# A mixture-of-experts block on one core: down weights laid out by pieces, no barrier behind the last round, the last norm inside the loop

## What is computed

```python
top_val, top_idx = lax.top_k(logits, TOP_K)
gates = jax.nn.softmax(top_val, axis=-1)
...
hid = xb @ w_mlp1[e] + b_mlp1[e]
glu = jnp.minimum(hid[..., ::2], SWIGLU_LIMIT)
lin = jnp.clip(hid[..., 1::2], -SWIGLU_LIMIT, SWIGLU_LIMIT)
act = glu * jax.nn.sigmoid(SWIGLU_ALPHA * glu) * (lin + 1.0)
return act @ w_mlp2[e] + b_mlp2[e]
...
out = jax.ops.segment_sum(y, slot_tok, num_segments=n + 1)[:n]
...
x = x + gt2 * rms_norm(ffn, g_post_ffn[l])
```

## Time and profile before

| | us |
|---|---|
| three runs: median (lowest, highest) | 1760.31 (1758.86, 1767.95) |
| the profiled execution | 1761.02 |
| its span, first to last instruction | 1759.2 |
| PE, PEld, DVE, ACT busy | 1606.3, 887.2, 620.0, 351.0 |
| L898 / L931 products, busy (2048 / 1024 records) | 456.5 / 234.1 |
| L920, second passes (128 records, 1157.4 to 1365.0) | 27.8 |
| loads of expert weights | 384, 1 MB each |
| tail, small ones: L2177 total, L1424 root, L2180 reciprocal | 0.16, 0.30, 0.17 |
| tail: a Square of a quarter with the read of its total (L1419) | 0.69 |

### The profile page before, as it was taken

One profiled execution on the slowest core, in us unless ns is written; L12 is line 12 of the kernel. 1 busy time (PEld: TensorE's weight loads), 2 busy tenths in 40 slices (PEclk: granted clock), 3 DMA queues, 4 the chain that ended last, 5 costly groups with the idle time before them and its releaser, 6 DMA issues. The chain is left out here.

```text
span 1759.2 us, 20527 instructions
## 1 busy us (share of the span) xinstructions
PE 1606.3 (91%) x7254; PEld 887.2 (50%) x7254; DVE 620.0 (35%) x1429; ACT 351.0 (20%) x647; POOL 0.2 (0%) x4
## 2 busy tenths in 40 slices
PE   1999899999999897879999988899999999999894
PEld 1888788788888674733333322233333333333222
DVE  5547762589720367232121111111112111221111
ACT  1124563332210124131111111101111111111102
POOL 0000000000000000000000000000000000000000
PEclk8999899999999998879999999999999999999998
DMA  9836673457863330229999999999999999999993
GB/s 399 343 126 245 266 284 132 153 224 295 366 255 127 124 131 1 96 86 380 416 416 416 415 417 416 417 416 417 416 417 400 383 383 416 416 417 415 417 415 127
DMA packets 93604, 545.46 MB, mean 310 GB/s; under 512 B 8944, under 2 KB 9456, under 8 KB 44304
## 3 DMA queue, kind: packets, MB, share of 16 engines
q1 hardware_dynamic: 92144, 540.74, 76.5%
q10 hardware_dynamic: 1312, 2.75, 0.4%
HBM read 542.41 MB, written 1.05 MB: 309 GB/s over the span
## 5 line engine op out<-in xcount | busy, mean ns | idle before, releaser
L898 PE MATMUL bank<-ring,scr 128*64 128x512 f32 x2048 | 456.5, 598 | 19.4 <-DMA ring<-in_w_mlp 19.2
L501 PE MATMUL bank<-hT,ring 128*128 128x256 f32 x1856 | 415.8, 385 | 24.5 <-ACT hT L1070 24.0
L501 PEld LDWEIGHTS bank<-hT,ring 128*128 128x128 f32 x1856 | 358.6, 194 | 79.6 <-issue 28.8
L898 PEld LDWEIGHTS bank<-ring,scr 128*64 128x64 f32 x2048 | 142.9, 137 | 314.5 <-issue 255.5
L931 PE MATMUL bank<-ring,hT 128*64 128x512 f32 x1024 | 234.1, 597 | 4.6 <-DMA ring<-in_w_mlp 3.5
L2090 DVE TENSOR_SCALAR scr<-bank 128x256 f32<-128x256 f32 x64 | 27.0, 422 | 396.4 <-PE bank L898 396.4
L931 PEld LDWEIGHTS bank<-ring,hT 128*64 128x64 f32 x1024 | 68.5, 136 | 143.6 <-issue 131.4
L2156 DVE COPY hT<-bank 64x512 f32<-64x512 f32 x32 | 22.2, 695 | 320.1 <-PE bank L931 290.2
L1359 ACT ACTIVATE scr<-scr 128x256 f32<-128x256 f32 x64 | 26.7, 417 | 503.8 <-DVE scr L2090 503.8
L1463 DVE SCALAR_TENSOR_TENSOR ring<-ring,cb 128x1024 f32<-128x1024 f32 x96 | 113.3, 1220 | 9.8 <-DMA cb<-in_cb 6.3
L646 PE MATMUL bank<-scr,ring 128*128 128x256 f32 x384 | 83.5, 379 | 1.6 <-ACT scr L1215 1.6
(11 more groups left out here) (365 smaller groups left out, 1288.4 us busy)
## 6 DMA issues: line engine op xcount, KB each, us to landing
ring<-in_w_mlp SPq DMA_DIRECT2D x384, 1024.0 KB, 20.1
ring<-in_w_in SPq DMA_DIRECT2D x28, 1024.0 KB, 20.4
ring<-in_ada_w SPq DMA_DIRECT2D x24, 1024.0 KB, 8.4
ring<-in_up SPq DMA_DIRECT2D x24, 1024.0 KB, 5.7
ring<-in_w_ada SPq DMA_DIRECT2D x24, 1024.0 KB, 7.5
ring<-in_down SPq DMA_DIRECT2D x12, 1024.0 KB, 13.9
ring<-in_w2in SPq DMA_DIRECT2D x6, 1024.0 KB, 9.5
ring<-in_w_out SPq DMA_DIRECT2D x4, 1024.0 KB, 8.0
```

The source lines that it names most:

```text
L501: ins = mm(b[:, 256 * j:256 * j + 256], v[:, k * 256 + j * 128:k * 256 + j * 128 + 128], rhs[:, k, :], start=(k == 0), stop=(k == 7))
L898: ins = mm(HID[0][n][64 * hf:64 * hf + 64, :], K.xe[0][x % 2][:, xo:xo + 64], v[:, o0:o0 + 512], start=False, stop=(k == 7), skip_group_ch ...
```

## The change

It has three parts. The down weights are laid out on the host by pieces, so that a partition's two rows lie together in one run of 8 KB. The barrier is taken only when another round follows: each engine reads the count at the loop's top and keeps whether more than 128 are left (`more`). And in the other arm of that branch, for the last round, stand the last norm and the stores, in a new form: the sums are squared and copied to SBUF by quarters, in the order in which `add_pair` finishes them; the scale is a diagonal matrix (`diag`) with which PE multiplies the unscaled sums, a product in place of a transpose. With it, the last expert's down products go to bank 3, and the counts of the next round are made at x = 31, inside the loop. Behind the arm the engines still go through the loop's test.

```diff
@@ -262,6 +262,7 @@
         self.aT = [[spare[:, 0:512], spare[:, 512:1024]], [carve(512), carve(512)]]
         self.ypair = [spare[:, 1024:1536], spare[:, 1536:2048]]
         self.ysb = carve(512)
+        self.diag = [self.w1[:, 0:128], self.w1[:, 128:256]]
         self.gTf = self.gT[0:32].rearrange("p a b -> p (a b)")
         self.HID = [[self.bank[0], self.bank[1]], [self.bank[2], self.bank[3]]]
         self.OUT = [[self.bank[4], self.bank[5]], [self.bank[6], self.bank[7]]]
@@ -379,8 +380,7 @@
         if layer == 0:
             v = self.a["w_mlp1"].rearrange("x (k p) n -> x k p n", p=128)
             return v[bass.ds(expert, 1), part].rearrange("x p n -> (x p) n")
-        v = self.a["w_mlp2"].rearrange("x (m k p) n -> x m p k n", p=128, k=2)
-        return v[bass.ds(expert, 1), part].rearrange("x p k n -> (x p) k n")
+        return self.a["w_mlp2"][bass.ds(expert, 1), part].rearrange("x p n -> (x p) n")
 
     def second_use(self, i):
 
@@ -397,6 +397,10 @@
 
     def down_at(self, x):
         return self.up_at(min(x + 1, NE - 1)) + 8 + 4 * (x == NE - 1)
+
+    def down_bank(self, x):
+
+        return self.bank[3 if x == NE - 1 else 2]
 
     def main_bank(self, key):
         return self.bank[self.main_at[key] % 3]
@@ -441,6 +445,7 @@
     e.sem_inc(S.loop_ring, 1)
     e.wait_ge(S.pos, 1)
     with e.While(lambda: rest_of(e, K) > 0):
+        more = rest_of(e, K) > 2 * CAP
         expert = {0: 0, 1: 1}
         for i in range(RING, len(K.moe)):
             x = K.moe[i][1]
@@ -452,22 +457,23 @@
             e.wait_ge(second, value)
             src = K.moe_source(i, expert[x])
             e.dma_start(K.slot(first + i, src, SLOT), src).then_inc(S.ring[(first + i) % RING], 16)
-        e.wait_ge(S.bar, 3)
-        for s in S.round:
-            e.sem_clear(s)
-        e.sem_clear(S.bar)
-        with e.If(rest_of(e, K) > 0):
+        with e.If(more):
+            e.wait_ge(S.bar, 3)
+            for s in S.round:
+                e.sem_clear(s)
+            e.sem_clear(S.bar)
             for i in range(RING):
                 src = K.moe_source(i, K.moe[i][1])
                 e.dma_start(K.slot(first + i, src, SLOT), src).then_inc(S.ring[(first + i) % RING], 16)
-        e.sem_inc(S.go_pe, 1)
-        e.sem_inc(S.go_act, 1)
-        e.sem_inc(S.go_dve, 1)
-
-    for c in range(4):
-        e.wait_ge(S.x, 20 + c + 1)
-        e.dma_start(K.out[:, 2 * c:2 * c + 2, :], K.xT[:, 2 * c:2 * c + 2, :]).then_inc(S.out, 16)
-    e.wait_ge(S.out, 64)
+            e.sem_inc(S.go_pe, 1)
+            e.sem_inc(S.go_act, 1)
+            e.sem_inc(S.go_dve, 1)
+        with e.Else():
+            for c in range(4):
+                e.wait_ge(S.x, 20 + c + 1)
+                e.dma_start(K.out[:, 2 * c:2 * c + 2, :], K.xT[:, 2 * c:2 * c + 2, :]).then_inc(S.out, 16)
+            e.wait_ge(S.out, 64)
+            e.wait_ge(S.m_left, 8)
 
 
 def rest_of(e, K):
@@ -928,7 +934,7 @@
             q, hf = kt % 4, kt // 4
             for oh in range(2):
                 g = 64 * (oh if c else oh ^ x % 2)
-                ins = mm(B[1 if c else 2][g:g + 64, :], K.aT[c][x % 2][:, 128 * q + 64 * hf:128 * q + 64 * hf + 64],
+                ins = mm((K.down_bank(x), B[1])[c][g:g + 64, :], K.aT[c][x % 2][:, 128 * q + 64 * hf:128 * q + 64 * hf + 64],
                          v[:, j * 1024 + oh * 512:j * 1024 + oh * 512 + 512], start=(kt == 0), stop=(kt == 7),
                          skip_group_check=True)
         return ins
@@ -1010,7 +1017,10 @@
                 e.wait_ge(S.m_aT, x)
                 if x == 1:
                     e.wait_ge(S.m_order, 1)
-                if x >= 2:
+                if x == NE:
+                    e.wait_ge(S.m_selT, NE)
+                    e.wait_ge(S.n_selT, NE)
+                elif x >= 2:
                     e.wait_ge(S.m_ypa, x - 1)
                     e.wait_ge(S.m_ypv, x - 1)
                 for m in range(3):
@@ -1027,21 +1037,25 @@
                 gates(x + 1)
                 second_block(x + 1)
         add_pair(NE // 2 - 1)
-        e.wait_ge(S.m_pair, NE)
-        e.sem_inc(S.bar, 1)
-        e.wait_ge(S.go_pe, 1)
-        e.sem_clear(S.go_pe)
-
-
-    for c in range(4):
-        if c == 0:
-            e.wait_ge(S.f_acc, 2)
-            e.wait_ge(S.f_sq, 2)
-        for j in range(2):
+        with e.If(more):
+            e.wait_ge(S.m_pair, NE)
+            e.sem_inc(S.bar, 1)
+            e.wait_ge(S.go_pe, 1)
+            e.sem_clear(S.go_pe)
+        with e.Else():
+
+            e.wait_ge(S.m_ypa, NE)
+            e.wait_ge(S.m_ypv, NE)
             for tt in range(2):
-                ins = e.transpose(B[c][:, 256 * j + 128 * tt:256 * j + 128 * tt + 128],
-                                  K.acc[:, tt, (2 * c + j) * 128:(2 * c + j + 1) * 128], ident)
-        ins.then_inc(S.f_tr, 1)
+                e.wait_ge(S.gain, 6 + tt)
+                for c in range(4):
+                    for j in range(2):
+                        ins = mm(B[c][:, 256 * j + 128 * tt:256 * j + 128 * tt + 128],
+                                 K.acc[:, tt, (2 * c + j) * 128:(2 * c + j + 1) * 128], K.diag[tt], start=True, stop=True,
+                                 skip_group_check=True)
+                    if tt:
+                        ins.then_inc(S.f_tr, 1)
+            e.wait_ge(S.m_left, 8)
 
 
 def scalar_program(e, K):
@@ -1405,27 +1420,39 @@
                 e.wait_ge(S.m_piece, K.down_at(x - 1) + 4)
                 if x >= 3:
                     e.wait_ge(S.m_pair, 2 * ((x - 1) // 2))
-                act(K.ypair[(x - 1) % 2][0:64, :], B[2][0:64, :], ACT.Copy).then_inc(S.m_ypa, 1)
+                act(K.ypair[(x - 1) % 2][0:64, :], K.down_bank(x - 1)[0:64, :], ACT.Copy).then_inc(S.m_ypa, 1)
             if x + 1 < NE:
                 second_block(x + 1)
-        table(ACT.Sqrt)
-        e.wait_ge(S.m_ypa, NE)
-        e.sem_inc(S.bar, 1)
-        e.wait_ge(S.go_act, 1)
-        e.sem_clear(S.go_act)
-
-    for tt in range(2):
-        for q in range(2):
-            ins = act(K.h4[:, tt, q * 512:(q + 1) * 512], K.OUT[tt][q][:, :], ACT.Square,
-                      accum_out=K.sm[:, 8 + 2 * tt + q:9 + 2 * tt + q])
-    ins.then_inc(S.f_sq, 1)
-
-    e.wait_ge(S.f_acc, 1)
-    act(K.sm[:, 2:4], K.sm[:, 0:2], ACT.Sqrt, bias=eps, scale=1.0 / D).then_inc(S.norm_rt, 1)
-    e.wait_ge(S.rstd, 6)
-    for q in range(2):
-        ins = act(K.acc[:, 1, q * 512:(q + 1) * 512], K.OUT[1][q][:, :], ACT.Identity, scale=K.sm[:, 5:6])
-    ins.then_inc(S.f_sq, 1)
+        with e.If(more):
+            e.wait_ge(S.m_ypa, NE)
+            e.sem_inc(S.bar, 1)
+            e.wait_ge(S.go_act, 1)
+            e.sem_clear(S.go_act)
+        with e.Else():
+
+            table(ACT.Sqrt)
+
+            def square(tt, q, v):
+                act(K.h4[:, tt, q * 512:(q + 1) * 512], v, ACT.Square,
+                    accum_out=K.sm[:, 8 + 2 * tt + q:9 + 2 * tt + q]).then_inc(S.f_sq, 1)
+
+            def halves(tt):
+
+                e.wait_ge(S.m_pair, NE - 1 + tt)
+                square(tt, 1, K.OUT[tt][1][:, :])
+                if tt:
+                    root(0)
+                e.wait_ge(S.f_acc, tt + 1)
+                square(tt, 0, K.acc[:, tt, 0:512])
+
+            def root(tt):
+                e.wait_ge(S.nsum, 21 + tt)
+                act(K.sm[:, 2 + tt:3 + tt], K.sm[:, tt:tt + 1], ACT.Sqrt, bias=eps, scale=1.0 / D).then_inc(S.norm_rt, 1)
+
+            halves(0)
+            halves(1)
+            root(1)
+            e.wait_ge(S.m_left, 8)
 
 
 def vector_program(e, K):
@@ -2147,48 +2175,67 @@
                 ts_(K.gpT[32:64], K.gpT[32:64], -2.0 * CAP, None, ALU.add)
                 ts_(posm, posm, -2.0 * CAP, None, ALU.add)
                 ts_(K.cntf, K.cntf, -2.0 * CAP, None, ALU.add).then_inc(S.m_left, 1)
+                e.wait_ge(S.m_left, 7)
+                e.tensor_copy(K.cnti[:, 0:32], K.cntf)
+                e.tensor_reduce(K.cnti[:, 32:33], K.cntf, AX.X, ALU.max).then_inc(S.m_left, 1)
             if x < NE:
                 second_activate(x)
             if x:
                 e.wait_ge(S.m_piece, K.down_at(x - 1) + 4)
                 if x >= 3:
                     e.wait_ge(S.m_pair, 2 * ((x - 1) // 2))
-                e.tensor_copy(K.ypair[1 - (x - 1) % 2][64:128, :], B[2][64:128, :]).then_inc(S.m_ypv, 1)
+                e.tensor_copy(K.ypair[1 - (x - 1) % 2][64:128, :], K.down_bank(x - 1)[64:128, :]).then_inc(S.m_ypv, 1)
             if x + 1 < NE:
                 turned_gates(x + 1)
                 many[x + 1] = crowded(e, K, x + 1)
                 second_block(x + 1)
-
-        e.wait_ge(S.m_left, 7)
-        e.wait_ge(S.m_ypa, NE)
-        e.wait_ge(S.m_pair, NE)
-        e.tensor_copy(K.cnti[:, 0:32], K.cntf)
-        e.tensor_reduce(K.cnti[:, 32:33], K.cntf, AX.X, ALU.max).then_inc(S.m_left, 1)
-        e.wait_ge(S.m_left, 8)
-        e.wait_ge(S.m_ypv, NE)
-        e.sem_inc(S.bar, 1)
-        e.wait_ge(S.go_dve, 1)
-        e.sem_clear(S.go_dve)
-
-
```

(68 more changed lines are left out.)

## The result

Over seven runs each, the changed kernel takes 1751.03 us (median, 1747.89 to 1753.33) and the kernel before 1763.05 (1756.65 to 1770.16): a ratio of 0.9929, 95% interval 0.9909 to 0.9950, or 12.5 us less, between 9 and 16. It is faster, by less than the 14.3 us of the sum, and the median lies at the upper end of the range (1742 to 1751). The profiled executions differ by less than the medians: 1751.07 against 1761.02, spans 1749.3 and 1759.2, so 9.9 us. The spread of the executions goes with the granted clock: of the 54 runs of the kernel before in the experiments' three groups, those with a mean clock of 0.969 or 0.970 took 1756.8 to 1760.0 us, and those with 0.964 or less 1762.2 to 1770.1.

The account below looks back on a forecast made before the run. It took transfers to bound the full stretches, PE the stretch between, and a stepwise tail the end. Terms -5.8+0.6+0-9.1 gave -14.3 us: 1746.7 from the profiled 1761.0, 1746.0 as median; range 1742 to 1751.

Parts of the forecast that it names:

- Term 1: MoE loop's down pieces in 8 KB rows: 0.065 us saved on each of 88 pieces that set the pace, -5.8 us.
- rivals A: Down-piece loads: the 4 KB runs cost nothing on the way, term 1's saving is given back, 1751.8 us; chance 0.08.
- C: Down-piece loads: only half of the 0.065 us is the runs' own, -2.9 for -5.8, 1748.9 us; chance 0.07.
- E: Down-piece loads: the new rows read worse, a piece comes 0.2 us later, 1769.4 us, slower; chance 0.03.
- Term 2: Loop's top, before the first gather: a second read of the count costs +0.6 us, bounds 0 to 1.
- Term 3: Last expert's down in another bank: PE's 0.99 us wait goes, but the last landing still decides, 0 us.
- term 4: Next round's counts made inside x = 31: two small DVE operations fall where DVE idles, 0 us.
- Term 5: Tail behind the last sums: 17.6 us become 4.5, less 4.0 for SP's way out, -9.1 us.
- Rival B: Tail: the clock falls before the diagonal products, last update 2.6 us later, 1748.6 us; chance 0.24.
- Rival D: Tail's branches: a second jump misses like the jump back, 3.2 us once more, 1749.2 us; chance 0.08.

Follow-up runs that it names:

- 2 KB runs: Changed kernel with a down piece in four runs of 2 KB for a partition: 1774.15 us (3 runs) against 1762.04 before.
- late read: Changed kernel with the count read at the round's end in all four engines, not at the loop's top: 1748.98 us, ratio 0.9920 to the kernel before.
- the layout alone: Kernel before with only the new down-weight layout added: 1755.15 us against 1761.44, ratio 0.9967.
- old layout: Changed kernel with the down weights back in two runs of 4 KB for a partition: 1756.29 us, ratio 0.9978 to the kernel before.
- wait behind: Changed kernel with SP's wait for the stores' landing moved behind the loop: 1749.38 us, ratio 0.9944 to the kernel before.
- both together: Changed kernel with the count read at the round's end and SP's store wait behind the loop: 1746.89 us against 1760.40 before, ratio 0.9925.

## Why the prediction was right, and where it was not

**Term 1, the layout (-5.8): right.** (88x0.065 is 5.7; the sum has 5.8.) It measured 5.7 and 5.3 us from piece 17, the distance of down pieces 2.485 as taken from the up pieces, the stretch from 819 shorter by 2.9 us (335.4 to 332.6 between the landings at its ends, forecast 2.9). In the last stretch the gain was 1.5 in this pair of profiles in place of 2.9: single landings there come 0.4 to 1.5 us late, now here and now there, in every profile. What makes them late is open. The Trainium skill's price (DMA: Bandwidth & Descriptors, "Why small descriptors are slow (HBM only)") would have made it 2.6; the 2 KB runs show 0.068 us for each 128 runs, more than twice that, and rivals A, C and E fall.

**Term 2, the second read (+0.6): the step that was mis-sized.** With the read alone added to the kernel before, it measured +2.4 us from piece 17; the other pairs that differ by it in the loop give 3.4 to 5.3 (changed against late read 5.3, against the layout alone 3.8, old layout against before 3.4, wait behind against both together 3.4). The read itself is 0.6: PE waits 2.6 us for its first gather in all eight kernels that have the read at the top, and 2.0 in the five others. What I left out is the clock. At 806 us the eight have 3.4 more us at 1.2 GHz; of the five others one has them, and it differs from a kernel without them only in the tail. A second fall at 1137, behind the wait of 2.28 us that stayed at full in the earlier trace rows, came in six of the eight and in that same one of the five. So that the read and the falls go together is shown by count. That the first steps of the round stand near an edge and 0.6 us tips them over is my reading, and how much of the 2.4 to 5.3 us is one execution's own is open: the times give 0 to 4 us for the read. "From 0 to 1" was too narrow a bound: the stretch was PE's, and half clock was in the view all the time.

**Term 3 (0) and term 4 (0): right**, the first with less than 0.1 us of cover; the rows had 0.5, or 0.2 with the earlier transfers.

**Term 5, the tail (-9.1): -7.9, by two errors.** From the last down piece to the first update the sum said 11.0 and it is 11.03. The way out behind the stores is there in series: from landing to end 3.7 us in place of 0.4, so 3.3 more and not 4.0. But "the other engines do the same earlier, beside it" was wrong as a price of nothing: their jumps fetch code over the same DMA engines that carry the stores, and the last store landed 1.9 us later: -9.1-0.7+1.9 = -7.9. A page of the Trainium skill (Runtime: NRT & Kernel Launch, "Instruction fetch mechanics") has the fetch as a DMA in a queue that the engine's sequencer drives itself; that it delays a store the trace and the experiment show.

**Rival B** did not happen in the profile of the changed kernel, and did in five of the eight kernels with the new tail and the gap unfilled: 1.2 to 1.6 us there, at the first update as at the last, and not 2.6: the clock stood at half for 3.4 us of the products and not for all of them (1730.5 to 1733.9 of 1729.4 to 1734.9 in the late read's profile). Rival D did not happen: one jump of 2.6 us and an exit of 0.3.

In sum, forecast against profile: term 1 5.8 and 4.3 (2.9 and 1.5), the read and the clock at the loop's start +0.6 and +1.7, the stretch that PE sets 0 and +0.5, the tail -9.1 and -7.9: -14.3 and -9.9. The 1.4 us that the last stretch lacks are the late landings above, with no cause shown.

## What to carry to other kernels

Where a piece's price can't be seen alone, a difference of two distances gives it to hundredths of a microsecond, and it counts only over the pieces whose landing something waits for. A jump back to a loop's top is a fetch over the DMA engines: put waits for the last stores behind the loop, so that the way out lies under their landing (3.0 us here in the profile, not resolved by the times), and look at what else lands while engines leave. A step of half a microsecond put ahead of a stretch that PE sets may cost more than itself if the clock has fallen near it; one pair of profiles does not price it: look at the granted clock of several.

## What the runs showed of the hardware that was not expected

The time of a load goes with the number of runs: 1 MB in runs of 8, 4 and 2 KB lands every 2.485, 2.553 and 2.694 us. While engines jumped (instruction packets of 0.93 and 0.48 us beside the store), one of the sixteen parts of the last store landed 1.9 us behind the others; with the jumps behind the landing it was on time. A wait of PE of the same 2.28 us left the clock at 2.4 GHz in some kernels and was followed by 1.2 GHz in others, and for two of them the programs differ only in the tail, behind both.
